# One decoder-trunk kernel, one rearrangement: the value projections of the first dilated group and of the block-sparse branch made in one pass

## The reference

```
h = rms_norm(x);  proj = h @ w_in            # D_MODEL 1024 -> 5120 columns: q, k, v of all heads, two gates
A: dilated causal attention, 3 groups of 4 heads (head size 64), (window, dilation) = (128,1), (512,4), (2048,16)
   group outputs combined by their softmax denominators
B: block-sparse causal attention, 4 heads: block 256, top-3 past blocks + own block (gating by mean key)
y = (sigmoid(gA) * (oA @ W_A) + sigmoid(gB) * (oB @ W_B)) @ w_out;   x = x + rms_norm(y)
h = rms_norm(x);  u = gelu(causal_dwconv3(h @ W_gate)) * (h @ W_up);  x = x + rms_norm(u @ W_down)
```

## Time and profile before

| | us |
|---|---|
| three runs | 3795.25, 3796.89, 3797.97 (median 3796.89) |
| profiled execution, whole | 3794.95 |
| its span on the slowest core (core 7) | 3793.6 |
| spans of the 8 cores | 3790.2 to 3793.6 |
| PE busy | 3708.5 (98%) |
| DVE, ACT, POOL busy | 2008.8, 1756.4, 876.3 |

### The profile page before, as it was taken

One profiled execution on the slowest core, in us unless ns is written; L12 is line 12 of the kernel. 1 busy time (PEld: TensorE's weight loads), 2 busy tenths in 40 slices (PEclk: granted clock), 3 DMA queues, 4 the chain that ended last, 5 costly groups with the idle time before them and its releaser, 6 DMA issues.

```text
span 3793.6 us, 55772 instructions; the slowest of 8 cores (3790.2 to 3793.6 us)
## 1 busy us (share of the span) xinstructions
PE 3708.5 (98%) x19888; PEld 1806.4 (48%) x19888; DVE 2008.8 (53%) x2985; ACT 1756.4 (46%) x3389; POOL 876.3 (23%) x1484
## 2 busy tenths in 40 slices
PE   5999999999999999999999999999999999999999
PEld 4644444444554444444465444444446544444444
DVE  4354666465346466646434646754643454675463
ACT  2457345254346635535334753543533475354351
POOL 2331332111133133211113223221111322331110
PEclk9999999999999999999999999999999999999999
DMA  6234788454323478864542358874542336796442
GB/s 151 29 77 72 154 172 162 115 99 90 84 35 74 74 164 181 147 170 78 123 95 53 57 93 170 176 133 128 78 106 52 56 59 108 157 193 120 101 69 73
DMA packets 304009, 410.38 MB, mean 108 GB/s; under 512 B 150704, under 2 KB 167344, under 8 KB 303728
## 3 DMA queue, kind: packets, MB, share of 16 engines
q0 software_dynamic: 118656, 190.89, 33.3%
q1 hardware_dynamic: 185088, 215.92, 20.8%
HBM read 500.56 MB, written 67.63 MB: 150 GB/s over the span
## 4 chain that ended last, share of the span: by engine, by line
PE 94%; DVE 3%; ACT 1%; issue 1%; DMA 1%; POOL 0%; SPq 0%; DVEq 0%; POOLq 0%; ACTq 0%
PE psum L396 35%; PE psum L1297 16%; PE psum L1025 12%; PE psum L643 11%; PE psum L551 6%; PE psum L676 5%; PE psum L620 5%; PE psum L965 3%; PE psum L707 1%; DVE s_arena L722 0%; DMA s_xr<-x 0%; ACT s_arena L716 0%; DVE s_arena L388 0%; DVE s_arena L997 0%; DVE s_hb L473 0%
## 5 line engine op out<-in xcount | busy, mean ns | idle before, releaser
L396 PE MATMUL psum<-s_hT,s_slabs 128*128 128x512 bf16 x5632 | 1223.9, 379 | 2.6 <-DVE s_arena L1258 2.6
L396 PEld LDWEIGHTS psum<-s_hT,s_slabs 128*128 128x128 bf16 x5632 | 551.4, 98 | 668.6 <-issue 5.3
L1297 PE MATMUL psum<-s_arena 128*128 128x512 bf16 x2816 | 609.1, 379 | 0.0
L1025 PE MATMUL psum<-s_hT,s_slabs 128*128 128x512 bf16 x2048 | 489.7, 379 | 0.4
L1247 DVE SCALAR_TENSOR_TENSOR s_arena<-s_arena,s_convw 128x512 f32<-128x512 f32 x352 | 264.2, 751 | 425.3 <-ACT s_arena L1239 425.2
L643 PE MATMUL psum<-s_hT,s_slabs 128*128 128x512 bf16 x2048 | 473.1, 379 | 12.0 <-DVE s_km L833 4.6
L1297 PEld LDWEIGHTS psum<-s_arena 128*128 128x128 bf16 x2816 | 275.6, 98 | 332.2
L424 ACT ACTIVATE s_hb<-psum 128x1024 bf16<-128x1024 f32 x128 | 131.0, 1024 | 524.0 <-PE psum L1297 344.5
L433 DVE SCALAR_TENSOR_TENSOR s_tz<-psum,s_stat,s_gpost 128x1024 f32<-128x1024 f32 x128 | 164.0, 1282 | 362.7 <-POOL s_stat L412 362.6
L976 ACT ACTIVATE s_arena<-psum 128x512 bf16<-128x512 f32 (+3 forms) x640 | 306.3, 542 | 86.3 <-PE psum L965 63.2
L676 PE MATMUL psum<-s_arena 128*128 128x128 bf16 (+2 forms) x1840 | 314.7, 264 | 7.6 <-DVE s_arena L997 2.4
(11 more groups left out here) (75 smaller groups left out, 3992.9 us busy)
## 6 DMA issues: line engine op xcount, KB each, us to landing
s_slabs<-w_in_r POOLq DMA_DIRECT2D x224, 256.0 KB, 4.8
xs<-s_xr SPq DMA_DIRECT2D x96, 512.0 KB, 3.3
s_xr<-xs SPq DMA_DIRECT2D x96, 512.0 KB, 5.5
s_slabs<-w_gate_r POOLq DMA_DIRECT2D x176, 256.0 KB, 4.4
s_slabs<-w_up_r POOLq DMA_DIRECT2D x176, 256.0 KB, 5.2
s_xr<-x SPq DMA_DIRECT2D x64, 512.0 KB, 6.3
s_arena<-w_down POOLq DMA_DIRECT2D x88, 256.0 KB, 6.3
y<-s_xr SPq DMA_DIRECT2D x32, 512.0 KB, 2.9
```

Source lines behind the costliest of these rows:

```text
L396: inst = nc.tensor.matmul(out, lhsT=l_, rhs=r_, start=(i == 0), stop=(i == n - 1))
L1025: inst = nc.tensor.matmul(ps[b], lhsT=buf[:, kc * 128:(kc + 1) * 128], rhs=hT[:, kc, tsl], start=(kc == 0), stop=(kc == 7))
L1297: inst = nc.tensor.matmul(ps[zb + n], lhsT=uT[:, kc, i * 128:(i + 1) * 128], rhs=wdn[kc][:, n * 512:(n + 1) * 512], start=(kc == 0), stop= ...
```

## The change

1. `v_joint` replaces `v_proj` for V0 at a mixer's start, and makes V0 and V3 together: for each token tile 8 matmuls of 128 x 512, over the columns of four slabs (12, 13, 22, 23), into one bank, then two copies of 256 columns by the same engine. V3 leaves units 2 and 3.
2. V1 and V2 are spread over units 0 to 2: half of V1 in unit 0, the rest of V1 at the head of unit 1 and a quarter of V2 at its end, the rest of V2 at the head of unit 2. Unit 3 keeps the query/key projection alone (its ratio stays at least 20).
3. The order of slabs follows; the prologue prefetches 4, 6 and 8 slabs in place of 2, 4 and 6.
4. `merge` gets a `lead`: 1.8 us of fill ahead of unit 0's first scores; -3.0 for `tail_out` beside the second half's gates (the fill starts later).
5. The mask multiplication of two tiles is written with (head, query) as one axis; group 2 gets a dense layout (`Pd16`) and a dense mask.

```diff
-def merge(main, *fills):
-    live = [[gen, ratio, 0.0] for gen, ratio in fills]
+def merge(main, *fills, lead=0.0):
+    live = [[gen, ratio, lead] for gen, ratio in fills]
...
+    run()
+    for cost in main:
+        for f in live:
+            f[2] += cost * f[1]
+        run()
...
+        def v_joint(l, banks, toks, waits):
+            ones = [ones_memset(Vb[G], waits) for G in (0, 3)]
+            ld = [load_w(l, c) for c in (12, 13, 22, 23)]
...
+            for tau in range(16):
+                b = banks.get()
+                PE.wait([x[1] for x in ld], hT_tok[tau])
...
+                for kc in range(8):
+                    w0 = ld[0][0][:, kc * 128:(kc + 1) * 128]
+                    rhs = bass.AP(tensor=w0.tensor, offset=w0.offset, ap=[list(w0.ap[0]), [1024, 4], [1, 128]])
+                    inst = nc.tensor.matmul(ps[b], lhsT=hT[:, kc, tau * 128:(tau + 1) * 128], rhs=rhs, start=(kc == 0), stop=(kc == 7))
+                tp = PE.do(inst)
+                q = evac_eng()
+                q.wait(tp, waits)
+                for i, G in enumerate((0, 3)):
...
+                    tc_ = copy_on(q, v6[:, :, 0:3:2, :], ps[b][:, 256 * i:256 * i + 256].rearrange("p (a b c) -> p a b c", a=2, c=64))
...
+                yield 1.77
...
-                drain(v_proj(l, 0, ALLB, vt[0], p_wait))
+                drain(v_joint(l, ALLB, (vt[0], vt[3]), p_wait))
...
-                    if sp == 0 and g2 > 0:
-                        fills.append(v_proj(l, g2, FB_, vt[g2], p_wait))
-                        total += 14.4
+                    if i == 0:
+                        vg = [v_proj(l, g_, FB_, vt[g_], p_wait) for g_ in (1, 2)]
+                        fills.append(take(vg[0], 7.0))
+                        total += 7.2
+                    elif i == 1:
+                        fills.append(vg[0])
+                        total += 7.2
+                    elif i == 2:
+                        fills.append(vg[1])
+                        total += 10.8
...
-                if i == 2:
-                    fills.append(take(vm, 7.0))
-                    total += 7.2
-                if i == 3:
-                    fills.append(vm)
-                    total += 7.2
+                    if i == 1:
+                        fills.append(take(vg[1], 3.4))
+                        total += 3.6
...
-                merge(dil_unit(g, sp, QK[i % 2], qt[(g, sp)], vt[g], acc_free, res), (fill, max(total, 20.0 if i == 3 else 0.0) / 6.9))
+                merge(dil_unit(g, sp, QK[i % 2], qt[(g, sp)], vt[g], acc_free, res), (fill, max(total, 20.0 if i == 3 else 0.0) / 6.9), lead=1.8 if i == 0 else 0.0)
...
-            merge(gates(l, 1, nt1, ob_done, FB3, p1_tok, mts1, wout_load), (tail_out(0, mts, mk2), 1.6))
+            merge(gates(l, 1, nt1, ob_done, FB3, p1_tok, mts1, wout_load), (tail_out(0, mts, mk2), 1.6), lead=-3.0)
...
-        slab_ring.prefetch(2)
+        slab_ring.prefetch(4)
```

More of the change, by code:

```diff
@@ L80, with run @@
 KB = 256
-def merge(main, *fills):
-    live = [[gen, ratio, 0.0] for gen, ratio in fills]
-    for cost in main:
+def merge(main, *fills, lead=0.0):
+    live = [[gen, ratio, lead] for gen, ratio in fills]
+    def run():
         for f in list(live):
-            f[2] += cost * f[1]
             while f[2] > 0:
@@ L576, in build @@
         Pd = [carve(o * KB, 512, BF16).rearrange("p (k h q) -> p k h q", k=2, h=2) for o in (68, 70, 72, 86)]
+        Pd16 = [carve(o * KB, 256, BF16).rearrange("p (k h q) -> p k h q", k=2, h=2) for o in (68, 70, 72, 86)]
         Pm = [carve(A_P + i * 256, 256, BF16) for i in range(6)]
@@ L695, in dil_unit @@
             head = g * 4 + 2 * sp
+            Pu = Pd if g < 2 else Pd16
             for step in range(8 + SKEW):
@@ L718, in dil_unit @@
                         bank_free[b] = [tE[-1]]
-                    dm = dmask[:, head:head + 2, :].rearrange("p (o h) q -> p o h q", o=1)
                     for (a, b, nq), te in zip(pieces, tE):
                         DVE.wait(te)
-                        tM = DVE.do(nc.vector.tensor_tensor(out=P[:, a:b, :, 0:nq], in0=P[:, a:b, :, 0:nq],
-                                                            in1=dm[:, :, :, 0:nq].to_broadcast([128, b - a, 2, nq]), op=ALU.mult))
+                        if b - a == 2:
+                            w = 2 * nq
+                            c0 = head * 256 if g < 2 else 2048 + 256 * sp
+                            p_ap = P.rearrange("p k h q -> p k (h q)")
+                            m_ap = dmask[:, :, :].rearrange("p (o a) b -> p o (a b)", o=1)[:, :, c0:c0 + w].to_broadcast([128, 2, w])
+                        else:
+                            p_ap = P[:, a, :, 0:nq]
+                            m_ap = dmask[:, head:head + 2, 0:nq]
+                        tM = DVE.do(nc.vector.tensor_tensor(out=p_ap, in0=p_ap, in1=m_ap, op=ALU.mult))
                         for k in range(a, b):
@@ L1362, in build @@
                 if t == 3:
-                    slab_ring.prefetch(4)
+                    slab_ring.prefetch(6)
                 if t == 9:
-                    slab_ring.prefetch(6)
+                    slab_ring.prefetch(8)
                 first.append(u)
@@ L1383, in build @@
             for l in range(n_layers):
-                rest, r_free = mixer(s, l, xs_tok, p_wait, (vt0, qt0) if s == 0 and l == 0 else None)
+                rest, r_free = mixer(s, l, xs_tok, p_wait, (vt0, vtm, qt0) if s == 0 and l == 0 else None)
                 ffn(s, l, xs_tok, rest, r_free)
@@ L1419, in _constants @@
             dmask[:, h, :] = np.where(valid, np.exp(-sl[h] * DILS[g] * np.where(valid, delta, 0.0)), 0.0)
+    d16 = dmask[:, 8:12, 0:128].copy()
+    dmask[:, 8:12, :] = 0.0
+    dmask[:, 8:10, :] = d16.reshape(128, 2, 256)
     tri = (np.arange(128)[None, :] >= np.arange(128)[:, None]).astype(np.float32)
```

26 lines of the change are left out of this document (18 added, 8 removed).

## The result

| | before | after |
|---|---|---|
| runs, us | 3795.25 to 3797.97 | 3810.24, 3811.38 |
| span of core 7, profiled run | 3793.6 | 3808.2 |
| ratio, with its 95% interval | | 1.0038 [1.0021, 1.0055] |

The change makes the kernel slower by about 14 us (0.38%), where 3796 and a range up to 3805 had been forecast.

The account below looks back on a forecast made before the run. PE, busy 98% of the span at full clock, was taken as the bound. The terms summed to -1.0 us on the profiled 3794.95, plus 1.94 to reach the median: 3795.9, say 3796; range 3784 to 3805.

Parts of the forecast that it names:

- a: Value projection, mixers 1 to 3: one wide matmul for two narrow ones, 384 pairs, -1.0 us.
- b: Start of mixers 1 and 3: PE's 1.32 us wait in V0 for a DVE copy goes, -2.6 us.
- c: Unit 0, four mixers: the lead of 1.8 covers the first scores' 0.87 us wait for a query/key copy, -3.3 us.
- f: Mixer 0: V3's 14.0 us of PE work moves into the prologue, which lengthens by 9.0; -5.0 us.
- d: First output product, four mixers: the lead of -3.0 covers its wait for the last gates, -4.0 us.
- g: Units that run out of fill, and V products waiting for new copies: 4.3 us a mixer, +17.2 in all.
- e: Units: one of three projections limited to banks 6 and 7 leaves, taking its share of 6.8 us of stalls; -2.3 us.
- the third part of g: Units 1 and 2: V products wait for the newest copies of V1 and V2, 0.5 us a mixer.
- The other two parts of g: Bare steps without fill at the ends of units 0 and 3: 1.4 and 2.4 us a mixer.
- figure of 131 ns: Rival on the wide value matmuls: 131 ns each, -45 us, 3751; chance 0.01.
- The slower one: Rival: ACT becomes the bound at unit ends, 6.4 us a mixer, 3804.3; chance 0.14.
- h. The rest: Mask product and layout, DVE and ACT room in unit 3, slab order, POOL's memsets at mixers' starts: 0 us.

Follow-up runs that it names:

- the stretched ratio: Changed kernel with the fill ratios of units 0 and 3 lowered so that fill lasts to the unit's end; ratio 1.0051 to the kernel before.
- mended by the memset: Changed kernel with POOL's memset of V2's ones issued at unit 1's head, as before, not at its end; ratio 1.0026 to the kernel before.
- V whole: Changed kernel with V1 given out whole in unit 0 and V2 whole in unit 1, as before the change; ratio 0.9998 to the kernel before.
- the leads alone: Kernel before with only the new `merge` and its two leads, 1.8 and -3.0; ratio 0.9985 to the kernel before.
- the narrow halves: Changed kernel with each wide group of the joint projection made as two narrow ones; single time 3824.3 us, on a slower chip.
- the version at 0.9969: Changed kernel with V1 and V2 whole, unit 3's query/key projection evenly paced, and normalisation multiplications between unit 4's masks; ratio 0.9969 to the kernel before.
- unit 3 evenly paced: Changed kernel with unit 3's query/key projection given out over 20 units of cost in place of 14; ratio 1.0043 to the kernel before.

## Why the prediction was wrong

Terms in us over four mixers, core 7, worked out from the table of stages and the length of the block-sparse part:

| term | predicted | measured |
|---|---|---|
| a wide pair | -1.0 | -1.0 (0.32 in each of three) |
| b, c in mixers 1 to 3 | -5.1 | -6.0 |
| f, with c in mixer 0 | -5.8 | -8.9 |
| d lead of -3.0 | -4.0 | -4.6 |
| g and e | +14.9 | +32.8 |
| the rest of the block-sparse part | 0 | +2.4, 1.7 of it in mixer 0 |
| sum | -1.0 | +14.7 |

The cause of the last +2.4 is open.

**The step that failed is the third part of g:** "V1 and V2 are now still being made while units 1 and 2 use them, and a V product waits for the newest copy: three times some 0.2 a mixer, 0.5". Those waits are there, three a mixer and 1.2 together (L710 for L393). But I looked only at who reads the copies, not at what stands ahead of them on DVE, nor at what else the moved groups bring: a memset on POOL, just ahead of additions that lie over a DVE mask product. Unit 2 cost +4.8 a mixer, 19.1 in all: 2.3 a mixer by the memset's place, with the clock spells behind the stall, 0.6 by the additions even so, and 1.9 that is mostly waits for V2's copies and of unit 3's first scores. I had costed that memset at the starts and in the prologue, and passed over it where it moved most. The trace of before held the warning: the mask line's longest was 1803 ns, in a product of 128x1024 that takes 0.69 us when nothing holds it (147.02 on core 7), so something could hold it for over a microsecond; I read the median, 426 ns, and wrote 0.

**The other two parts of g** were right in kind and near in size: waits of 1.1 us at both ends, unit 3 2.3 to 2.8 us longer than its work where 2.4 was worked out. At unit 0 the stretched ratio took 1.5 off where 1.4 was expected. Unit 4 added 0.2 to 0.8 that I had not foreseen, with the multiplications of L847 standing ahead of its first mask.

**e** gave nothing, and its premise was wrong. Of the 6.8 us that I had split off, unit 0 held 3.2 and unit 1 3.5 (core 7, before); V3's groups, in the last third of units 2 and 3, didn't wait for a copy once. So V3 had no stalls to give back. All the waits of narrow groups, before and after, lie 2.6 to 8 us behind a unit's start, where the value groups stand first in the fill. The change emptied that place in unit 0 of its waits and filled it in unit 2: with the stall there mended by the memset, V copies are still waited for 7.6 us; with V whole 5.3.

**a, b, c, d** held; b and c together by 0.9 better. That c holds is partly luck, as the leads alone show. The Trainium skill's figure of 131 ns for such a matmul ("TensorE: Matmul & The Clock Gate", section "Back-to-back issue gap") would have given 45 us; the pace of 216 ns and the 0.32 us of the narrow halves rule it out here.

**f** was too dear by 3 us on core 7. On core 1 the wide groups on the chain from 45 us on take 1.90, as PE stays at full clock there; only two earlier ones take 3.5 (3.53 is one). First scores came at 90.2 on core 7 (91.15 on core 1), forecast 92 in place of 83.3. The prologue varies, though: over the eight cores the first scores come 8.2 us later in the mean, and not 6.9 as on core 7, and the other versions with this prologue had them between 89.2 and 94.4 on core 7, 91.6 in the mean. So about half of these 3 us is the luck of one run.

**The rivals.** The slower one gave the sign and nearly the time (3804.3), but not the place: it had ACT as the bound at the ends of units 0 and 3, and those cost what the forecast said. The loss came from DVE and POOL in unit 2. No rival touched unit 2. "h. The rest", 0, holds for the mask's layout.

## What to carry to other kernels

When a producer is moved, list everything that its first step issues on every engine, and lay each of these beside what runs there, not only the moved matmuls. Narrow groups with two banks waited at the heads of units and not at their ends; at the head of unit 2 one late copy became a stall of PE of 2.5 us, and in some mixers a slower clock behind it. Before counting a stall as a gain, look which of the groups has it. A fill's ratio paces every chain that shares it, so test a new ratio with the small transfers in mind and give slow side work its own place, as the version at 0.9969 does.

## What the runs showed that I had not expected

- POOL's additions hold DVE's product of two bf16 operands: 2.59 and 2.71 us for one of 128x512 that takes 0.42 to 0.43 alone, and up to 3.00 (this kernel's longest) for one of 128x1024 that takes 0.69. The view of the line, after, core 1 (shortest, median, longest in ns):

```profile
L764 DVE TENSOR_TENSOR s_arena<-s_arena,s_dmask x232: 283/427/3004, 92.6 to 3071.5; 128x512 bf16<-128x512 bf16 x52, 128x1024 bf16<-128x1024 bf16 x44, 128x256 bf16<-128x256 bf16 x20
```

  The copies out of PSUM, DVE's own (0.42 at 149.28, in the block of additions from 148.67) and ACT's, ran at their usual length beside the same additions, and beside POOL's memset (1085.78 to 1087.61, core 7) a mask product took its 0.43. The Trainium skill has the rule ("SBUF — State Buffer", section "SBUF: two separate sides"): a DVE operation with two SBUF inputs and a GpSimd operation that reads SBUF take a shared pair of ports for a whole instruction each, and the other stands. The rows agree, and each held product at the head of unit 2 ended 0.3 us behind the end of an addition. The rule alone does not say why the product had to let a second addition pass in one case.
- The same wait of 2.5 us at the head of unit 2 was followed by a spell at 1.2 GHz in mixers 0 and 3 and not in 1 and 2 of core 7; the spell cost 1.5 us (34.4 against 32.9). Which mixers have it changes from core to core and run to run: 18 of the 32 units 2 of this execution took 34.4, and on core 7 all four did with unit 3 evenly paced. With the wait at 0.97 none of 32 had it.
- ACT's table load takes 1.28 us and moves onto the path by a single copy ahead of it.
